# Modulation by rows: the adaptive matrix laid out with its columns on the partitions

## What is computed

```
cond = silu(c)                                  # [1, 1024]
for layer in range(2):
    mod = cond @ ada_w[layer] + ada_b[layer]    # [1024] @ [1024, 6144]
    sh1, sc1, g1, sh2, sc2, g2 = split(mod, 6)
    h = rms_norm(x, norm_mix[layer]) * (1 + sc1) + sh1
    y = even_mixer(h, ...) or odd_mixer(h, ...)
    x = x + g1 * y
    h = rms_norm(x, norm_mlp[layer]) * (1 + sc2) + sh2
    x = x + g2 * ((relu(h @ mlp_w1[layer]) ** 2) @ mlp_w2[layer])
```

## Time and profile before

| | us |
|---|---|
| median of 3 runs | 1430.33 |
| the profiled execution | 1430.49 |
| its span, first to last instruction | 1428.70 |
| TensorE matmuls busy | 1342.2 (94%) |
| TensorE weight loads busy | 1105.1 (77%) |
| VectorE busy | 941.8 (66%) |
| ScalarE busy | 657.2 (46%) |
| GpSimd busy | 109.8 (8%) |
| mean granted TensorE clock | 0.984 |

### The profile page before, as it was taken

One profiled execution on the slowest core, in us unless ns is written; L12 is line 12 of the kernel. 1 busy time (PEld: TensorE's weight loads), 2 busy tenths in 40 slices (PEclk: granted clock), 3 DMA queues, 4 the chain that ended last, 5 costly groups with the idle time before them and its releaser, 6 DMA issues.

```text
span 1428.7 us, 16545 instructions
## 1 busy us (share of the span) xinstructions
PE 1342.2 (94%) x6684; PEld 1105.1 (77%) x6684; DVE 941.8 (66%) x1249; ACT 657.2 (46%) x886; POOL 109.8 (8%) x156
## 2 busy tenths in 40 slices
PE   6999999999989999999798898999998988999998
PEld 6767888887867788888598776888886866788886
DVE  4857677766675777775757857776766776554444
ACT  4544533333463543333365454454544554454542
POOL 1010000000020000000114300000002320000000
PEclk9999999999999999999998999999999998999999
DMA  9505577773712667776153213767673530355550
GB/s 363 199 1 206 209 308 293 295 279 126 272 60 77 227 245 294 292 295 220 61 183 104 90 56 120 293 240 290 238 292 114 181 118 1 118 206 188 188 184 30
DMA packets 40236, 269.87 MB, mean 189 GB/s; under 512 B 4544, under 2 KB 4560, under 8 KB 11872
## 3 DMA queue, kind: packets, MB, share of 16 engines
q1 hardware_dynamic: 37712, 259.31, 48.8%
q0 software_dynamic: 2304, 8.46, 1.6%
q10 hardware_dynamic: 144, 1.05, 0.2%
HBM read 267.75 MB, written 1.05 MB: 188 GB/s over the span
## 4 chain that ended last, share of the span: by engine, by line
PE 81%; DVE 11%; ACT 3%; issue 2%; POOL 1%; DMA 1%; SPq 0%; POOLq 0%; ACTq 0%; DVEq 0%
PE ps L1441 23%; PE ps L1443 23%; PE ps L1442 23%; PE ps L1466 4%; PE ps L1551 2%; DVE WB L1764 2%; PE ps L1527 1%; PE ps L1454 1%; PE ps L1426 1%; ACT WB L1564 1%; DMA RAW<-W 1%; DVE st L2027 1%; DVE X L2037 1%; DVE st L1957 1%; DVE X L2040 1%
## 5 line engine op out<-in xcount | busy, mean ns | idle before, releaser
L1764 DVE TENSOR_TENSOR WB<-RAW,WB 128x2048 fp32r<-128x2048 f32 (+4 forms) x210 | 453.2, 2161 | 267.4 <-ACT WB L1564 267.3
L1564 ACT ACTIVATE WB<-RAW 128x2048 fp32r<-128x2048 f32 (+4 forms) x210 | 379.7, 1810 | 232.8 <-PE ps L1443 219.6
L1441 PE MATMUL ps<-WB,XTH 128*128 128x512 f32 (+3 forms) x1176 | 457.9, 389 | 20.0 <-DVE XTL L1769 13.0
L1443 PE MATMUL ps<-WB,XTL 128*128 128x512 f32 (+3 forms) x1176 | 448.2, 381 | 0.0
L1442 PE MATMUL ps<-WB,XTH 128*128 128x512 f32 (+3 forms) x1176 | 447.5, 381 | 0.0
L1441 PEld LDWEIGHTS ps<-WB,XTH 128*128 128x128 f32 x1176 | 223.8, 190 | 60.6 <-DVE XTL L1769 13.3
L1443 PEld LDWEIGHTS ps<-WB,XTL 128*128 128x128 f32 x1176 | 222.9, 190 | 38.4
L1442 PEld LDWEIGHTS ps<-WB,XTH 128*128 128x128 f32 x1176 | 223.8, 190 | 34.9
L1441 PE MATMUL ps<-WB,HTH 128*128 128x512 f32 (+1 forms) x452 | 178.4, 395 | 2.5 <-DVE HTL L1845 2.0
L1443 PE MATMUL ps<-WB,HTL 128*128 128x512 f32 (+1 forms) x452 | 177.7, 393 | 0.0
L1442 PE MATMUL ps<-WB,HTH 128*128 128x512 f32 (+1 forms) x452 | 177.6, 393 | 0.0
(11 more groups left out here) (177 smaller groups left out, 1043.4 us busy)
## 6 DMA issues: line engine op xcount, KB each, us to landing
RAW<-W SPq DMA_DIRECT2D x220, 1024.0 KB, 4.9
RAW<-W SPq DMA_DIRECT2D x14, 768.0 KB, 4.3
RAW<-W SPq DMA_DIRECT2D x12, 728.0 KB, 6.0
VEC<-vecd POOLq DMA_DIRECT2D x10, 512.0 KB, 7.2
RAW<-W SPq DMA_DIRECT2D x8, 512.0 KB, 3.5
RAW<-W SPq DMA_DIRECT2D x4, 576.0 KB, 3.6
GB<-xTd ACTq DMA_DIRECT2D x1, 1024.0 KB, 7.8
X<-xd SPq DMA_DIRECT2D x1, 1024.0 KB, 16.1
```

The source lines that it names most:

```text
L1441: eng.matmul(ps, xh, hi[:, j, c0:c0 + cw], start=first and j == 0, stop=False)
L1443: op = eng.matmul(ps, xl, hi[:, j, c0:c0 + cw], start=False, stop=last and j == n - 1)
L1564: return eng.activation(dst, src, f, **k)
L1764: eng.tensor_tensor(WB[:, it["raw"], 0:w], RAW[:, it["raw"], 0:w], WB[:, it["high"], 0:w].bitcast(F32), ALU.subtract).then_inc(*up("wl", n))
```

## The change

`ada_w` is laid out transposed. In an item, 128 of the columns of `ada_w` lie on the partitions, and the 1024 rows (the axis that is summed) lie along the free axis; an item holds two such groups of columns, a chunk has two items, as before. The bytes, the number of items, their place in the order and their buffers stay. `cond` becomes a tile of its own, [128, 1024]: all 1024 values on every partition, loaded by a DMA that repeats the vector 128 times (512 KB into SBUF), the last that GpSimd issues at the start. ScalarE's Silu runs over all of it and waits for this load in place of `colv`.

VectorE does an item in two `tensor_tensor_reduce` instructions of 128 x 1024, one for each group of columns: product with `cond`, written over the raw values, and sum along the row, starting from the bias, straight into a column of `modc`. `ACC` and its rotation, `total` on TensorE, the addition on VectorE, `flush` and all its calls and the bank that each sum took are gone. `cond` has the size that `ACC` had.

```diff
-            def total(f, a, layer, c, n, b, after):
...
-                for q in range(4):
-                    op = eng.matmul(banks[b][:, q:q + 1], ACC[:, a, q * 128:q * 128 + 128], ones[:, 0:1],
-                                    start=True, stop=True)
-                op.then_inc(*up("sum", f))
...
+            eng.dma_start(cond[:, :], bc(condd)).then_inc(*landed("cond_in", 0))
...
             def setup():
-                on.wait_ge(*at("colv", 0))
-                act(cond, cond, ACT.Silu).then_inc(*up("cond", 0))
+                on.wait_ge(*at("cond_in", 0))
+                act(cond[:, :], cond[:, :], ACT.Silu).then_inc(*up("cond", 0))
...
-            def ada(it, after):
-                n, a = it["id"], it["acc"]
-                view = RAW[:, it["raw"], :].rearrange("p (k w) -> p k w", k=4)
+            def ada(it):
+                n, c = it["id"], it["col"] // 128 + it["a"] // 2
+                view = RAW[:, it["raw"], :].rearrange("p (q k) -> p q k", q=2)
                 on.wait_ge(*at(f"raw{it['raw']}", n))
                 on.wait_ge(*at("cond", 0))
-                for e in after:
-                    on.wait_ge(*at(*e))
-                for j in range(4):
-                    kt = it["a"] + j
-                    if kt == 0:
-                        op = eng.tensor_scalar(ACC[:, a, :], view[:, j, :], cond[:, kt:kt + 1], None, ALU.mult)
-                    else:
-                        on.wait_ge(*at("ada", (n, j - 1) if j else it["prev"]))
-                        op = eng.scalar_tensor_tensor(out=ACC[:, a, :], in0=view[:, j, :], scalar=cond[:, kt:kt + 1],
-                                                      in1=ACC[:, a, :], op0=ALU.mult, op1=ALU.add)
-                    op.then_inc(*up("ada", (n, j)))
-
-            def total(f, a, layer, c, n, b, _):
                 on.wait_ge(*at("colv", 0))
-                on.wait_ge(*at("sum", f))
-                eng.tensor_tensor(modc[:, layer, c * 4:c * 4 + 4], banks[b][:, 0:4],
-                                  colv[:, K_ADAB + layer * 48 + c * 4:K_ADAB + layer * 48 + c * 4 + 4], ALU.add
-                                  ).then_inc(*up("mod", f))
+                for q in range(2):
+                    b0 = K_ADAB + it["layer"] * 48 + c + q
+                    op = eng.tensor_tensor_reduce(view[:, q, :], view[:, q, :], cond[:, :], 1.0, colv[:, b0:b0 + 1],
+                                                  ALU.mult, ALU.add, modc[:, it["layer"], c + q:c + q + 1])
+                op.then_inc(*up("ada", n))
...
+        if name == "ada_w_2":
+            w = w.T.reshape(4, 128, k).transpose(1, 0, 2).reshape(128, 8, -1)
+        else:
+            w = w.reshape(k // 128, 128, -1).transpose(1, 0, 2)
```

More of the change, by code:

```diff
@@ L147 @@
     wait_ge = then_inc = dma_start = matmul = transpose = activation = tensor_copy = tensor_tensor = same
-    tensor_scalar = scalar_tensor_tensor = tensor_reduce = reciprocal = memset = max = match_replace = same
+    tensor_scalar = scalar_tensor_tensor = tensor_tensor_reduce = tensor_reduce = reciprocal = memset = max = match_replace = same
     bn_stats = bn_aggr = same
@@ L175, in wait_ge, with program @@
             self.past[id(sem)] = value
-def program(nc, W, xd, xTd, pTd, posd, pos2d, colvd, cstd, cstbd, vecd, sgwd, smalld, out):
+def program(nc, W, xd, xTd, pTd, posd, pos2d, colvd, cstd, cstbd, vecd, sgwd, smalld, condd, out):
     with ExitStack() as ctx:
@@ L201, in program @@
         SQ = sb("SQ", [128, 512])
-        ACC = sb("ACC", [128, 2, 512])
+        cond = sb("cond", [128, 1024])
         with nc.sbuf_tensor("TB", [128, 4, 2, 2, 64], F32) as TB:
@@ L228, in program @@
         ones = cst[:, C_ONE:C_ONE + 128]
-        cond = colv[:, K_C:K_C + 8]
         MH = cst[:, C_MH:C_MH + 1]
@@ L289, in program @@
             it["id"] = n
-        cur = {"chunk": 0, "item": 0, "load": 0, "ahead": 0, "pairs": 3, "acc": 0, "sum": 0, "id": 0, "col": 0, "turn": 0, "buf": 0,
-               "ada": None, "lag": False}
+        cur = {"chunk": 0, "item": 0, "load": 0, "ahead": 0, "pairs": 3, "id": 0, "col": 0, "turn": 0, "buf": 0,
+               "lag": False}
         bufs = [(n, []) for n in range(NBUF)]
         low = []
-        acc_free = [[], []]
-        ada_done = []
         mod_w = {}
@@ L325, in advance @@
                 if it["name"] == "ada_w_2":
[L326 to L336, removed]
+                    do("ada", it)
+                    mod_w.setdefault((it["layer"], it["col"] // 1024), []).append(("ada", it["id"]))
+                    bufs.append((it["raw"], [("ada", it["id"])]))
                 else:
@@ L354, in used @@
             loads()
[L356 to L366, removed]
         def chunk_items(name):
@@ L705, in norm_mod @@
         def norm_mod(layer, k, after):
-            assert len(mod_w[(layer, 3 * k)]) == 2 and len(mod_w[(layer, 3 * k + 1)]) == 2
+            assert len(mod_w[(layer, 3 * k)]) == 4 and len(mod_w[(layer, 3 * k + 1)]) == 4
             do("mod_scale", layer, k, mod_w[(layer, 3 * k + 1)])
@@ L948, in gain @@
         def gain(layer, k, hf):
-            assert len(mod_w[(layer, 3 * k + 2)]) == 2
+            assert len(mod_w[(layer, 3 * k + 2)]) == 4
             if hf == 0:
@@ L1553, in values @@
                 op.then_inc(*up("pv", u["id"]))
-            parts = dict(mm=mm, sum=total, turn=turn, halves=halves, ffn_turn=ffn_turn, modulate=modulate,
+            parts = dict(mm=mm, turn=turn, halves=halves, ffn_turn=ffn_turn, modulate=modulate,
                          sel_score=sel_score, gating=gating, gain=gain, scores=scores, values=values)
@@ L2142, in diff_norm @@
                                   ).then_inc(*up("diff_norm", t))
-            parts = dict(low=low, x0=x0, setup=setup, ada=ada, sum=total, turn=turn, halves=halves,
+            parts = dict(low=low, x0=x0, setup=setup, ada=ada, turn=turn, halves=halves,
                          ffn_turn=ffn_turn, mod_scale=mod_scale, modulate=modulate, rope_in=rope_in,
@@ L2226 @@
             [a["ada_b_2"].reshape(96, 128), np.stack([a["norm_mix_2"], a["norm_mlp_2"]], 1).reshape(32, 128),
[L2227 removed]
+             a["sgu_b"].reshape(16, 128)]).T),
         "cstd": cst,
@@ L2233 @@
         "smalld": np.concatenate([a[n].reshape(-1) for n, _ in SMALL]),
+        "condd": np.ascontiguousarray(a["c_2"][0]),
     }
```

12 lines of the change are left out of this document (1 added, 11 removed).

## The result

| | before | changed kernel |
|---|---|---|
| median us | 1430.15 (1429.73 to 1430.45, 4 runs) | 1407.82 (1405.67 to 1409.89, 4 runs) |
| the profiled execution | 1430.49 | 1406.22 |
| its span | 1428.70 | 1404.30 |
| TensorE matmuls, weight loads busy | 1342.2, 1105.1 | 1317.6, 1081.6 |
| VectorE busy | 941.8 | 918.9 |

The ratio is 0.9844, 95% interval 0.9825 to 0.9863: 22.3 us less. Two later measurements of the same two kernels gave 0.9859 (0.9843 to 0.9875) and 0.9823 (0.9809 to 0.9836), with medians of 1410.97 and 1405.00 us.

A forecast was written before the change was run, and what follows sets the result against it. TensorE's instruction count was taken to bound the networks: 1430.49 - 20.7 (23 sums) - 2.3 (one sum with its wait) = 1407.5 us, all else costed at nothing. Range 1404.5 to 1418, the forecast's own 1404.5 to 1411.

The forecast's parts named there:

- part 1: TensorE in the networks: 24 sums leave; 23 give 0.90 us each, one with its wait 2.3, together 23.0 us.
- The wait for `ACC`: TensorE at 905.86 us: 1.18 us idle before one sum goes with it, 2.3 us in all.
- Part 2: VectorE's modulation: 96 new instructions at 1.4 us replace 141.5 us of work, 7 us less busy; hidden, costs nothing.
- The limit of 2.07 us: VectorE in first-kind chunks: it keeps up while a new instruction takes under 2.07 us.
- Part 3: Loads in the networks: needed rate rises from 295 to 309 GB/s; no load starts later, cost nothing.
- Part 4: Start of the kernel: the larger `cond` load and Silu arrive in time, cost nothing; bounds 0 to 2.6 us.
- The boundaries: Outside the networks: nothing removed or added, so no change, plus or minus 1 us.
- Half rate: Rival, VectorE: new instruction takes 2.29 or 2.49 us and bounds first-kind chunks; 1422 to 1435 us, chance 0.07.
- two passes: Rival, VectorE: product and then sum take 2.64 us, first-kind chunks 1.4 us longer; 1444 us, chance 0.05.
- The new wait: Rival, first-kind chunks: loads hold at 295 GB/s or a `high` or `low` comes late; 1411 to 1422 us, chance 0.10.
- That the sums might have overlapped: Rival, TensorE: sums overlapped weight loads and cost less; at least 19.0 us should go, 1411.5 us; no chance given.

The follow-up runs named there:

- a group of 1.9 us: Changed kernel with a further plain product of 128 x 512 behind each tensor_tensor_reduce on VectorE: 1411.15 us, ratio 0.9866.
- one of 2.46: Changed kernel with a further plain product of 128 x 1024 behind each tensor_tensor_reduce on VectorE: 1424.82 us, ratio 0.9963.
- four and eight: Changed kernel with 24 groups of four, or of eight, fp32 matmuls put back on TensorE: 1433.51 us (ratio 1.0022) and 1456.46 us (1.0181).

## Why the prediction was right

**The bound and part 1.** The reading that TensorE's instruction count ends the networks held: 17.87 became 17.00 (predicted 16.97), 23.89 became 23.03 (22.99). Each chunk gave 0.87 instead of 0.90 us. The wait for `ACC` went with its sum: the distance from the first to the second copy of the third network shrank from 26.19 to 23.01, 3.2 us, which is the 2.3 of that sum and 0.87 of the next. Predicted 23.0 us, found 22.0 in the three networks. With the sums alone taken out the networks gave 23.1, so the price of the sums was right, and the term that is missing in the working is one that takes 1.1 us back. Of the missing 0.03 to 0.04 us a chunk the runs show the origin only by elimination: with the sums gone and the old VectorE instructions kept the period is 16.97, with the new instruction 17.01; with the sums it is 17.87 and 17.92. In chunks of the second kind it is 22.95 against 23.03, twice as much. The new instruction isn't the cause, for the same 0.08 us stand in the fourth network, which carries no modulation at all. Two copies there that lie three chunks apart, before and after:

```profile
1301.93 1.09 ACT L1564 ACTIVATE HTH<-ps 128x512 fp32r<-128x512 f32 x2 [3.91 <-PE ps L1466]
...
1370.81 1.09 ACT L1564 ACTIVATE HTH<-ps 128x512 fp32r<-128x512 f32 x2 [3.91 <-PE ps L1466]
```

```profile
1277.09 1.09 ACT L1528 ACTIVATE HTH<-ps 128x512 fp32r<-128x512 f32 x2 [3.91 <-PE ps L1430]
...
1346.22 1.09 ACT L1528 ACTIVATE HTH<-ps 128x512 fp32r<-128x512 f32 x2 [3.91 <-PE ps L1430]
```

That is 22.96 and 23.04 us a chunk. By the starts in TensorE's order of time the whole difference lies in the 144 matmuls with `HTH` and `HTL`: their mean step is 232.4 ns in the kernel before and in the one with its sums taken out, and 234.2 or 234.3 ns in all ten profiles that have the changed layout of `cond` and `colv`. The matmuls with `XTH` and `XTL` take 230 ns in both. The change made `colv` narrower by eight columns, and `HTH` and `HTL` are allocated behind it, `XTH` and `XTL` ahead of it. So their place in SBUF may be the reason; no run tests that.

**Part 2.** 1.4 us was 1.28 and a readout of 0.08. VectorE's busy time fell by 23 us, not 7, because I summed durations at 1.4 us. The price of an instruction in a queue is its step from start to start, here 1.21: 141.5 - 96 x 1.21 = 25 us. An item holds the engine for 2.4 us, not 2.8. It cost nothing either way, as said. The limit of 2.07 us, worked out from durations, was not crossed by a group of 1.9 us, and crossed by one of 2.46; by the steps it lies at about 2.3.

**The Trainium skill's half rate** ("Vector Engine (DVE) Microarchitecture Reference", section "Points that are easy to get wrong") is not what happens here. The rows of `scalar_tensor_tensor` with two fp32 tensors in SBUF, 751 ns for 512 elements and 1282 for 1024, contradict it. The new instruction takes 1280 ns for 1024 elements with its sum, 1.25 ns each with all overhead. The trace calls it CUSTOM_DVE_ANT_0, so it may not be of the shape that the rule speaks of. The other rule of the Trainium skill ("VectorE: DVE Perf Modes", section "Two Vector instructions with no wait between them"), that the accumulator's readout is an instruction of its own, agrees: 96 of 84 ns.

**Part 3.** 309 GB/s, as worked out; no load became late.

**Part 4.** Nothing, as said. ScalarE in order of time after; `cond` arrives 0.44 us after ScalarE is ready for it, and the next wait hides that:

```profile
19.14 1.06 ACT L1528 ACTIVATE cond<-cond 128x1024 f32<-128x1024 f32 x1 [0.44 <-DMA cond<-condd]
22.18 0.27 ACT L1528 ACTIVATE SIN<-SQ 128x80 f32<-128x80 f32 x1 [1.98 <-DVE SQ L1769]
```

**The boundaries.** The term of plus or minus 1 us was too small. Outside the networks the first pair of spans differs by 24.4 - 22.0 = 2.4 us: with rounding 0.5 at the start, 0.1 between the first two networks, 2.5 of the jump at 699 to 714 us, and 0.8 lost again behind the third network, of which the slower matmuls with `HTH` and `HTL` are the larger part. In the medians part of this was given back, at 135, 1070 and 1220 us in some executions. So 1407.8 beside a forecast of 1407.5 is closer than the working deserves, and that is luck: the networks' sum was 1 us too high, a jump of 2 us that nobody forecast came beside it, and the clock moves the total by 3 us either way.

**The rivals.** Half rate and two passes fell with the duration of 1280 ns. The run with a whole product more, at the price of an instruction at half rate, came to 1425 us, inside the 1422 to 1435 given for that rival. Its bound was named rightly, but the number holds only by two errors that offset each other: the first kind lost less than the working had, since that went by durations and kept a wait of 0.4 us that vanished, and the third network lost 5.0 us where it had nothing. The new wait didn't come: TensorE waits for nothing between 150 and 320 us in the changed kernel. That the sums might have overlapped is refuted by the linear price of four and eight.

## What to carry to other kernels

Where one engine is busy without a gap and each small instruction has its step in the chain, moving such instructions to an engine with room gives back their full steps, however short they look beside the rest; read the step from the chain, not the duration. A plain fp32 matmul with 128 x 128 weights and one moving column cost 0.22 us here, as much as one with 512 columns in fp32r, so a reduction over partitions by ones is dear in a row of full matmuls, and laying the data out so that the sum runs along the free axis does away with it. Before handing the work on, find the price at which the other engine becomes the bound: here between 1.9 and 2.46 us for an instruction that takes 1.21. When a gain is right in its total, look for it place by place: here two kernels with the same median had theirs in different places.

## What the runs showed of the hardware

- On VectorE a product of two fp32 tensors with a sum along the row, 128 x 1024, takes 1280 ns and 84 ns for the readout; the plain product of the size takes 1220 to 1225.
- On TensorE an fp32 matmul with 128 x 128 weights and one moving column costs 0.22 us in a full stream, with four or with eight in a group, and leaves two records. A matmul of 512 columns with fp32r operands has a step of 0.23 us and leaves one.
- The step of the same fp32r matmuls of 512 columns differs by 1.8 ns between two builds of the program (232.4 and 234.2 ns with `HTH` and `HTL` as weights), the same in each profile of a build. Over a chunk of 48 of them that is 0.08 us.
- One program's executions lie up to 7.4 us apart (1404.96 to 1412.35). The spans of the three profiles are 1404.3, 1410.5 and 1403.1 us. In the longest the granted clock is at its lower level for some microseconds at 135, 1070, 1135 and 1220 us and in the others not; the periods are equal to 0.02 us in all three. A comparison of kernels that differ by less than 4 us needs many runs or the ledger of two traces.
